# Top-256 selection of five indexer tiles: a threshold found bit by bit in place of rounds of eight maxima

## The reference, cut to what matters

```python
s = relu(einsum('bqhd,bsd->bqhs', q_idx, k_idx) * IDX_DIM ** -0.5)
score = einsum('bqhs,bqh->bqs', s, w_idx * IDX_HEADS ** -0.5)
score = where(key_pos <= query_pos, score, -inf)
_, idx = lax.top_k(score, 256)        # ties: the lower index first
# attention of 6 heads over the 256 keys of idx
```

## Time and profile before

| | |
|---|---|
| median of 3 runs | 2902.53 us (2900.31 to 2904.22) |
| the profiled execution | 2905.52 us, its span 2903.7 us |
| PE busy | 2791.5 us, 96% |
| DVE busy | 1187.3 us, 41% |
| ACT, POOL busy | 903.1 us, 31%; 1023.4 us, 35% |
| L2300 + L2302 (maxima and replacing, x176 each) | 162.6 + 159.5 us |
| granted PE clock, mean | 0.979 of full |

### The profile page before, as it was taken

How to read it: one execution, slowest core, us unless ns; L and a number is a source line. 1 busy time by engine, 2 the same in 40 slices (tenths; PEclk the granted TensorE clock), 3 DMA queues, 4 the chain that set the end, 5 groups by cost and what they waited for, 6 DMA issues and landing times.

```text
span 2903.7 us, 41142 instructions
## 1 busy us (share of the span) xinstructions
PE 2791.5 (96%) x16908; PEld 2170.1 (75%) x16908; DVE 1187.3 (41%) x2813; ACT 903.1 (31%) x1701; POOL 1023.4 (35%) x447
## 2 busy tenths in 40 slices
PE   7999998899999999998999999999999999999998
PEld 5766675667777777775887778888888888887887
DVE  6979997556533333335345011111112121114423
ACT  5322413552333434334123222222222222214112
POOL 2542472133322222223541433333333323333542
PEclk8999998999999999999999999999999999999999
DMA  4110021131211111112221111111111111114211
GB/s 111 42 28 24 23 71 57 39 98 41 67 40 38 48 51 52 52 44 88 66 69 56 57 44 37 44 45 44 37 47 49 37 45 44 44 37 146 66 51 65
DMA packets 221334, 155.56 MB, mean 54 GB/s; under 512 B 25254, under 2 KB 207948, under 8 KB 221020
## 3 DMA queue, kind: packets, MB, share of 16 engines
q1 hardware_dynamic: 210076, 122.55, 14.6%
q10 hardware_dynamic: 11072, 30.39, 2.9%
HBM read 133.45 MB, written 19.47 MB: 53 GB/s over the span
## 4 chain that ended last, share of the span: by engine, by line
PE 51%; DVE 1%; issue 1%; ACT 1%; DMA 0%; ACTq 0%; DVEq 0%
PE proj L904 14%; PE proj L906 14%; PE proj L905 14%; PE out L1423 2%; PE score L1371 1%; PE score L1401 1%; PE score L1380 1%; PE proj L944 1%; PE out L906 0%; PE out L905 0%; PE out L904 0%; PE out L1390 0%; DMA y_scratch<-arena 0%; DVE arena L2343 0%; DVE arena L2470 0%
## 5 line engine op out<-in xcount | busy, mean ns | idle before, releaser
L904 PE MATMUL proj<-act_hi,w_hi 128*128 128x512 f32 x2560 | 1034.9, 404 | 10.4 <-ACT hT L1846 4.4
L906 PE MATMUL proj<-act_hi,w_lo 128*128 128x512 f32 x2560 | 1006.2, 393 | 0.0
L905 PE MATMUL proj<-act_lo,w_hi 128*128 128x512 f32 x2560 | 1005.7, 393 | 0.0
L777 POOL TENSOR_TENSOR w_hi<-w_raw,ones 128x1024 fp32r<-128x1024 f32 x175 | 420.6, 2403 | 1596.9 <-PE proj L906 1594.8
L904 PEld LDWEIGHTS proj<-act_hi,w_hi 128*128 128x128 f32 x2560 | 486.8, 190 | 123.6 <-issue 17.7
L906 PEld LDWEIGHTS proj<-act_hi,w_lo 128*128 128x128 f32 x2560 | 485.7, 190 | 105.4
L905 PEld LDWEIGHTS proj<-act_lo,w_hi 128*128 128x128 f32 x2560 | 487.2, 190 | 96.2 <-issue 0.2
L779 POOL TENSOR_TENSOR w_lo<-w_raw,w_hi 128x1024 fp32r<-128x1024 f32 x175 | 432.2, 2470 | 13.7
L1846 ACT ACTIVATE arena<-proj 128x512 f32<-128x512 f32 x236 | 175.9, 754 | 669.3 <-PE proj L906 645.3
L2470 DVE SCALAR_TENSOR_TENSOR arena<-arena,score 128x256 f32<-128x256 f32 (+1 forms) x192 | 76.1, 427 | 719.0 <-PE score L1371 677.3
L1872 ACT ACTIVATE arena<-score 128x512 f32<-128x512 f32 (+3 forms) x264 | 115.9, 487 | 199.6 <-PE score L1232 199.2
(11 more groups left out here) (268 smaller groups left out, 2879.7 us busy)
## 6 DMA issues: line engine op xcount, KB each, us to landing
w_raw<-dil_w_in_dram SPq DMA_DIRECT2D x80, 512.0 KB, 3.7
w_raw<-fox_w_in_dram SPq DMA_DIRECT2D x32, 512.0 KB, 4.1
w_raw<-w_in_dram SPq DMA_DIRECT2D x23, 512.0 KB, 3.7
y_scratch<-arena ACTq DMA_DIRECT2D x21, 512.0 KB, 3.5
act_lo<-y_scratch SPq DMA_DIRECT2D x21, 512.0 KB, 6.0
arena<-decay_scratch ACTq DMA_DIRECT2D x16, 512.0 KB, 5.7
w_raw<-ple_w_gate_dram SPq DMA_DIRECT2D x16, 512.0 KB, 3.7
arena<-x_dram SPq DMA_DIRECT2D x12, 512.0 KB, 4.8
```

The lines of the kernel that those rows point to most:

```text
L777: pool.tensor_tensor(hi, raw, one.unsqueeze(1).broadcast_to([P, KB, P]), ALU.mult).then_inc(w_hi_done, 1)
L904: pe.matmul(bank, hi, a_hi, start=first, stop=False)
L905: pe.matmul(bank, hi, a_lo, start=False, stop=False)
L906: return pe.matmul(bank, lo, a_hi, start=False, stop=last)
```

## The change

Tiles 3 to 7 take `threshold` in place of the rounds; tile 2 keeps its rounds, now in `lowest`. A row's threshold is built as an fp32 number: the row's sign is decided by one count of the elements >= 0 (`side`, +-0.5, by which the row is scaled), eight counts find the exponent, 23 the mantissa bits. A count is one `tensor_scalar` over the row, which compares with `cand` and adds up, starting from `short`; its full-size output goes to the mask's place as scratch. Each count is followed by narrow instructions of 1 to 24 columns that form the next candidate. Then the floor is subtracted, the elements above it are counted, ties get a running number by a scan, and the mask is written. Every instruction waits for the one before it. `beside(i, r)` is called after the same round numbers: 0 after the first count, 1 to 8 after the exponent counts, 9 to 31 after the mantissa counts. Two MEMSETs of one column are added at the start of DVE's program.

```diff
+        halving, met, weights = G.take(2), G.take(24), G.take(24)
+        side, short, cand, got, over, floor_ = (G.take(1) for _ in range(6))
...
+            dve.memset(halving[:, 0:1], 0.5).then_inc(IX["top"], 1)
+            dve.memset(halving[:, 1:2], 0.0).then_inc(IX["top"], 1)
...
-            top = 0
+            top = 2
...
+            def threshold(i, w, z):
+                nonlocal top
+                flag = maskb[:, mask_offset(i):mask_offset(i + 1)]
+                def small(ins):
+                    nonlocal top
+                    ins.then_inc(IX["top"], 1)
+                    top += 1
+                    dve.wait_ge(IX["top"], top)
+                def count(least, need, into, op=ALU.is_ge):
+                    small(dve.tensor_scalar(flag, z, least, need, op, ALU.add, accum_out=into))
+                dve.wait_ge(IX["top"], top)
+                small(dve.memset(met, 0.0))
+                small(dve.memset(cand, 2.0))
+                count(0.0, -float(TOPK), got)
+                beside(i, 0)
+                small(dve.tensor_scalar(side, got, 0.0, 0.5, ALU.is_ge, ALU.subtract))
+                small(dve.tensor_scalar(short, side, float(w - 2 * TOPK + 1), -(w + 1) / 2, ALU.mult, ALU.add))
+                small(dve.tensor_scalar(z, z, side, None, ALU.mult))
+                for r in range(8):
+                    count(cand, short, got)
+                    up, down = (2.0 ** (64 >> r), 2.0 ** -(64 >> r)) if r < 7 else (1.0, 0.5)
+                    small(dve.tensor_scalar(got, got, 0.0, up - down, ALU.is_ge, ALU.mult))
+                    small(dve.scalar_tensor_tensor(cand, got, down, cand, ALU.add, ALU.mult))
+                    beside(i, 1 + r)
+                small(dve.tensor_scalar(cand, cand, 2.0 ** 127, None, ALU.min))
+                small(dve.scalar_tensor_tensor(weights[:, 0:1], cand, 2.0 ** -126, cand, ALU.is_ge, ALU.mult))
+                small(dve.tensor_tensor_scan(weights[:, 1:24], halving[:, 0:1].broadcast_to([P, 23]),
+                                             halving[:, 1:2].broadcast_to([P, 23]), weights[:, 0:1], ALU.mult, ALU.add))
+                for k in range(1, 24):
+                    small(dve.scalar_tensor_tensor(flag[:, 0:k + 1], met[:, 0:k + 1], 0.0, weights[:, 0:k + 1], ALU.is_ge, ALU.mult,
+                                                   accum_out=cand))
+                    count(cand, short, met[:, k:k + 1])
+                    beside(i, 8 + k)
+                small(dve.scalar_tensor_tensor(flag[:, 0:24], met, 0.0, weights, ALU.is_ge, ALU.mult, accum_out=floor_))
+                small(dve.tensor_scalar(z, z, floor_, side, ALU.subtract, ALU.mult))
+                count(0.0, -float(TOPK), over, ALU.is_gt)
+                small(dve.tensor_scalar(flag, z, 0.0, None, ALU.is_equal))
+                small(dve.tensor_tensor_scan(flag, ones[:, 0:1].broadcast_to([P, w]), flag, over, ALU.mult, ALU.add))
+                small(dve.scalar_tensor_tensor(flag, z, 0.0, flag, ALU.is_equal, ALU.mult))
+                small(dve.tensor_tensor(flag, z, flag, ALU.is_lt))
+                dve.tensor_scalar(flag, flag, NEG, None, ALU.mult).then_inc(IX["sel"], 1)
...
                 if i == 2:
...
+                    lowest(i, w, scores)
                 else:
                     dve.wait_ge(IX["diag"], i - 2)
-                row = scores[:, 0:w] if i > 2 else scores[:, 0:w][:, ::-1]
-                for r in range((TOPK if i > 2 else w - TOPK) // 8):
-                    dve.wait_ge(IX["top"], top)
-                    dve.max(top8, scores[:, 0:w]).then_inc(IX["top"], 1)
-                    dve.wait_ge(IX["top"], top + 1)
-                    dve.match_replace(row, top8, row, -3e38).then_inc(IX["top"], 1)
-                    top += 2
-                    beside(i, r)
-                dve.wait_ge(IX["top"], top)
-                dve.tensor_scalar(maskb[:, mask_offset(i):mask_offset(i + 1)], scores[:, 0:w], -2e38, NEG,
-                                  ALU.is_gt if i > 2 else ALU.is_lt, ALU.mult).then_inc(IX["sel"], 1)
+                    threshold(i, w, scores[:, 0:w])
```

More of the change, by code:

```diff
@@ L2279, in _, with lowest @@
             dve.wait_ge(IX["wi"], 2)
-            top = 0
+            top = 2
+            def lowest(i, w, scores):
+                nonlocal top
+                row = scores[:, 0:w][:, ::-1]
+                for r in range((w - TOPK) // 8):
+                    dve.wait_ge(IX["top"], top)
+                    dve.max(top8, scores[:, 0:w]).then_inc(IX["top"], 1)
+                    dve.wait_ge(IX["top"], top + 1)
+                    dve.match_replace(row, top8, row, -3e38).then_inc(IX["top"], 1)
+                    top += 2
+                    beside(i, r)
+                dve.wait_ge(IX["top"], top)
+                dve.tensor_scalar(maskb[:, mask_offset(i):mask_offset(i + 1)], scores[:, 0:w], -2e38, NEG, ALU.is_lt, ALU.mult)\
+                   .then_inc(IX["sel"], 1)
```

## The result

The changed kernel takes 2942.8 us (median of 4, 2941.0 to 2943.4) where the kernel before takes 2903.0 (2900.3 to 2904.2) beside it: 1.0138 times, 95% interval 1.0125 to 1.0151, or +39.8 us. The forecast was 2949 in a range of 2909 to 2972. The profiled span is 2940.9 us for 2903.7.

A forecast was written before the change was run, and what follows sets the result against it. VectorE was taken to set the end of this phase, with PE nearly full afterwards. Steps of +12, +8, +8, +2, +4, +10 and +2 made +46 on 2902.5, so 2949 us, range 2909 to 2972.

The forecast's parts named there:

- Step 2: Ends of tiles 4 and 5: ACT's scaling waits for the later mask and stalls PE, +8 each, +2 for low clock.
- step 3: Tile 6's eleven rounds with chunks: rounds beside POOL's head sums and splits take 2.45 us for 1.48, +4.
- step 4: Tile 6's other 21 rounds and tail: 62 us with waits for POOL, before 52, +10.
- step 5: Tile 7: 65.5 us free, 18 for held instructions, some 5 for POOL waits; 89 for 87.4, +2.
- Free costs: VectorE with nothing in the way: count 1.34 us at 1024 columns, narrow instruction 0.19, mantissa round 1.62; tile 7 62.7 for 83.3.
- Rival A: Counts go at the double rate and take the lock too: about 15 us more than the forecast, 2964; chance 0.18.
- Step 1: Tile 3 and GLA's start: held instructions make chunk 0 about 9 us late, rounds to chunk 2 add 3, +12.
- the clock after the stall: After the stalls at the ends of tiles 4 and 5: a few us at lower clock, +2 for both.
- POOL backlog out of tile 6's tail: In tile 7: waits of POOL instructions for the tail of tile 6, some 5 us.
- the wait for the pool outputs: PE's 8.1 us wait for the pool outputs in tile 7 was to grow to about 20.
- Rivals B: Only wide instructions are held up, those of 1 to 24 columns slip through: +6, 2909 us; chance 0.12.
- C: GpSimd holds nobody up; masked sums beside busy POOL take 0.3 us: not slower, 2900 or 2896 us; chance 0.10.

The follow-up runs named there:

- experiment 1: Changed kernel, all five tiles by threshold, with narrow instructions reading one SBUF tensor each (masked sums as two one-column tensor_scalar): 2916.2 us, 1.0056 against the kernel before.
- Tiles 6 and 7 alone: Threshold as in the changed kernel on tiles 6 and 7 only, old rounds on 3, 4 and 5: 2905.4 us, +3.4 against the kernel before.
- tiles 4 and 5 alone: Threshold as in the changed kernel on tiles 4 and 5 only, old rounds on 3, 6 and 7: 2930.0 us, +26.8 against the kernel before.
- experiment 2: Changed kernel with the tail cut short, leaving out the choice among equal scores by a running count: 2911.9 us, 1.0040 against the kernel before.

## Why the prediction was right, and where its steps were off

The cause was right: two-input instructions, however narrow, wait for GpSimd's running one, and the tails stand before ACT's scaling. The time was 6 below the forecast. That it came so near is in part luck: steps 2 and 3 were 5 us too low, step 4 was 4.5 and step 5 was 7 us too high. By steps:

- **Free costs.** A count with its read and gap takes 1.38 us at 1024 columns (457.73 to 459.11) for 1.34, a narrow instruction 0.15 to 0.16 and a gap of 0.03 for 0.19, and a free mantissa round 1.59 (459.11 to 460.70) for 1.62. These terms stood. Rival A is out: no count is held (31 of tile 7's 33 in experiment 1 are at 1.33 or 1.34, two at 1.22).
- **Step 1 (+12)**: tile 3's mask at 143.4 for 141, chunk 0 12.3 us late and chunk 2 11.8. The sum held, its parts did not: 9 us were forecast at chunk 0 and 3 more up to chunk 2, and PE's stall for `chunk_keys` was 4.8 and not 1.3.
- **Step 2 (+8, +8, +2)** and **step 3 (+4)**, together +22, measured +27 (chunk 31 39.5 late, less the 12.3). PE's restart after tile 4 is 20.3 late, after tile 5 28.9: the stalls are 8 and 8.6. From there to chunk 31 it is 10.6 more, not 4 + 2. Tiles 6 and 7 alone are 3.8 late at chunk 31, which is step 3. Most of the rest is the clock after the stall, the mis-sized term: what the granted clock lacks, added up over 2 us windows from PE's restart to chunk 31, is 8.9 us for 3.1 before, an estimate of 5.8 where 2 were charged for both stalls. With tiles 4 and 5 alone it is 6.4, and there chunk 31 is 3.6 us later than the restart was (21.4 for 17.8); so part of the 5.8 comes only with tile 6's held rounds. Windows of the changed kernel after the stall,
```profile
326.00:336.00 10.00, 6.27 (x15) 4.33 (x16) 7.42 (x15) 4.66 (x10) 2.37 (x1) 0.50 0.07 20
336.00:346.00 10.00, 9.94 (x36) 5.82 (x34) 6.68 (x20) 3.73 (x9) 0.13 (x1) 0.84 0.00 0
346.00:356.00 10.00, 10.00 (x36) 7.12 (x34) 6.86 (x17) 0.06 (x1) 2.23 (x1) 0.75 0.00 0
```
and of the kernel before at the same work:
```profile
298.00:308.00 10.00, 9.94 (x39) 6.22 (x39) 8.37 (x16) 4.66 (x10) 6.87 (x3) 1.00 0.19 52
308.00:318.00 10.00, 9.94 (x41) 6.20 (x40) 9.58 (x16) 3.73 (x9) 2.40 (x1) 1.00 0.00 1
318.00:330.00 12.00, 11.19 (x39) 7.17 (x38) 11.45 (x20) 5.56 (x15) 5.14 (x3) 0.76 0.01 1
```
  From its restart at 329.73 PE is full, but at 0.50 (1.2 GHz) until 336, and low again (0.50) from 346 to 350. VectorE is busy 6.7 and 6.9 of 10 us in the second and third window, so it isn't its work that is late. The kernel before has one low stretch of its own, 0.50 from 326 to 330. Why the clock falls a second time near 345, with PE busy 9.94 of the 10 us from 336, no run here tells.
- **Step 4 (+10)** measured +5.5 (58.7 us for tile 6 after chunk 31, where it was 53.2; predicted 62 for 52, the end of the mask before being 383.6 and not 382.6). Ten of its 21 masked sums were held, nine were expected, for 9.5 us, as expected. The tail (L2341 to L2347 without the count) took 13.1 us for 5.8 free, 7.3 of waiting where seven times 1.5 were charged. The free part is 58.7 - 9.5 - 7.3 = 41.9 for 42.6.
- **Step 5 (+2)** measured -5 (81.2 us, where it was 86.2; predicted 89 for 87.4). Of the tile's 32 narrow two-input instructions 17 were held, for 15.2 us, for 22 and 18; the 5 us charged for a POOL backlog out of tile 6's tail didn't come. 81.2 - 15.2 = 66.0 is the free part, 65.5 in the prediction. L842 (5.8 us each time) was counted as a full holder, and for two inputs it holds only in the first 1.1 us of each of its two instructions. With fewer holds before (7,26) the wait for the pool outputs was 11.0 and not "about 20": that sign failed with the same term.
- **Rivals B and C** fell with the masked sum of two columns that takes 2.24 us. Alone, tiles 6 and 7 cost 3.4 us and not the 16 of steps 3 to 5.

What the prediction did not see is the balance: the part of the tail that experiment 2 leaves out is worth 31 us, more than the held narrow instructions (27).

## What to carry to other kernels

Before a chain of narrow VectorE steps is put beside a busy GpSimd, write each so that it reads one column and takes the rest as per-row scalars; with two inputs, or with 7 or 8 columns, each cost up to one GpSimd instruction here. Price a selection by its last few instructions if another engine waits for its result, and by its rounds if nobody does: the same threshold cost 27 us on the two tiles with a waiting consumer and 3 on the two without, where its one-input form gained 8. A part that stands on one engine's path can be worth nothing alone (tile 7: -1) and pay with its neighbour (tiles 6 and 7: -8), here because the neighbour brings forward a piece that PE waited 6 us for.

## What was not expected of the hardware

- A one-input tensor_scalar of 7 or 8 columns is held by GpSimd like one with two inputs (11 of 32, 18.9 us), and one of a single column never (32 of 32 at 0.15 to 0.16, and 270 at their free times in experiment 1). A single column with two inputs is held (L2333, 2.0 us in the mean of five). The Trainium skill ("VectorE: DVE Perf Modes", section "What auto-detection actually checks") lets a one-source instruction take the double rate with two ports if the outermost dimensions other than one of source and destination are even or equal. The rows agree as to which are held: 7 and 8 are equal on both sides, and one column has no such dimension. That the double rate is what holds them is not shown by itself.
- How long GpSimd holds depends on both forms: L841/L842 (one tensor read, 64 partitions, 2.85 us) held the 7- and 8-column tensor_scalar until its end, but narrow instructions with two inputs only until 1.12 to 1.14 us after its start (six of six); the twelve that came later passed at 0.16 to 0.17 us. GpSimd's instructions with two inputs held both until their end, on 64 partitions as on 128 (453.59 + 2.24 above). The Trainium skill ("SBUF — State Buffer", section "Who interferes with whom") has a two-input instruction contend with any GpSimd instruction that reads SBUF; for this GpSimd instruction the rows agree for its first 1.1 us and differ for the rest, and the measurement decides. Whether the one tensor read or the operation makes the difference, and what ends after 1.1 us, wasn't tried.
- A comparison with an added-up result runs at one column a cycle (1332 ns for 1024 columns) where the same comparison without the sum takes 693, and it isn't held.
- A per-row scalar operand adds 0.06 us to a one-column instruction (154, 214, 273 ns for none, one and two).
